# Inverse and transposed inverse in opposite halves of the partitions (a WKV/delta-rule chunk solver on one NeuronCore)

## The chip, the cores and the metric

One core of one Trainium2 chip runs the whole program. The metric is device time of one execution in microseconds; the median of three runs of the kernel before is 2838.22 us (2836.29 to 2838.88).

## What is computed

Two layers of a hybrid block on 256 context and 256 image tokens, all in float32: a mixer with three branches (latent attention, an mLSTM and an RWKV-7 recurrence), a gated merge, and a mixture of 64 experts. The change touches the third branch only. Its reference is a scan over tokens, four heads of 64, forward and backward:

```
def step(s, inp):
    r_t, w_t, k_t, v_t, kk_t, a_t = inp
    sa = jnp.einsum('bhij,bhj->bhi', s, -kk_t)
    s = (s * w_t[..., None, :] + sa[..., :, None] * (kk_t * a_t)[..., None, :]
         + v_t[..., :, None] * k_t[..., None, :])
    return s, jnp.einsum('bhij,bhj->bhi', s, r_t)
```

The kernel computes it in chunks of 64 tokens, for which it needs, per chunk and head, the inverse of a 64x64 unit triangular matrix.

## The kernel before, in words

The 512 tokens are 8 chunks (`NC`) of 64. The four heads are two pairs, `pr` 0 and 1; the two heads of a pair lie in partitions 0 to 63 and 64 to 127 (`each_head`, L908). All tiles of pair 0 have the name `arena` in the profile, those of pair 1 `ring`. `rw_pe` (L911), `rw_act` (L1058) and `rw_dve` (L1121) are the programs of TensorE, ScalarE and VectorE for this branch; each engine runs its own list in order and they meet at semaphores. The branch runs once per layer `l` and direction `d`, so four times.

A product of this branch is 64x64 by 64x64: its operands' partitions choose the rows of the 128x128 array, its output's partitions choose the columns, so it takes one quarter of the array. A float32 product is two MATMUL records, each with its own LDWEIGHTS record; below, one such record is called a pass.

For each `(l, d)`, in this order on TensorE:

- Scores (L947 to L969), masked into `MB` and `MK` by VectorE (L1188).
- The inverse. `X` is the inverse built so far, `XT` its transpose, `NL` the blocks of the matrix that level `v` takes in (`blocks`, L1181). At `v` = 0 TensorE transposes `NL` (L981, with `ident`, 16 products a pair), VectorE makes `X` = I - `NL` (L1195, both operands in SBUF) and `XT` = I - transposed `NL` (L1199, from PSUM). At `v` = 1 to 5 TensorE forms `NL`ᵀ`XT` (L981, 16 products a pair), ScalarE copies it to `ZT` (L1101), and TensorE makes the two updates: L996 for `X` and, at `v` below 5, L998 for `XT`, 16 products each a pair, in the order chunk, head, L996, L998. VectorE subtracts them: `XT` in L1210, `X` in L1212, pair 0 first, then pair 1. L981 of the next level waits for `XT` of its pair (`xt_is`).
- Between L981 and the updates TensorE does a piece of other work, the modulation rows of this or the next layer: `turn` (L326, 8 passes) and `rows` (L313, 16 passes, weights from the DMA ring). Layer 0 has such pieces at all levels, layer 1 `rows` at levels 1 to 3 and `turn` at 1 to 4.
- The scan over chunks, 8 steps. One step: `RH` (L1012, L1013) in each pair, copied with a minus by ScalarE for pair 0 (L1106) and VectorE for pair 1 (L1216); `UU` = `X`·`RH` (L1018), copied (L1108, L1218); the next state (L1024, L1025, L1028), scaled and copied to `ST` (L1112, L1222); the outputs (L1037 to L1039). The next step's L1012 waits for `ST`.

In this kernel every product of the branch has its operands and its output in the same half of the partitions, so only two quarters of the array are ever used: low rows with low columns, and high rows with high columns.

Of the kernel before, what the change touches and what calls it, by code (L numbers as in the profile page):

```python
# [7 lines left out]
ALU = mybir.AluOpType  # L8
# [19 lines left out]
C = 64  # L28
NC = T // C
# [128 lines left out]
def bcast(ap, axis, n):  # L158

    a = ap.unsqueeze(axis)  # L160
    shape = list(a.shape)
    shape[axis] = n
    return a.broadcast_to(shape)


def build(nc, xin, consts, smalls, wsm, wst, wexp, out):
    es = ExitStack()
    with es:
# [22 lines left out]
        ps = [es.enter_context(nc.psum_tensor(f"bank{i}", [P, 512], F32)) for i in range(8)]  # L191
# [11 lines left out]
        def cn(name, n, o=0):  # L203
            return CT[:, CN[name] + o:CN[name] + o + n]
# [4 lines left out]
        ident, ones, bd = cn("ident", P), cn("ones", P), cn("bd", P)  # L209
# [147 lines left out]
        def queries_from(l):  # L357

            return 0 if l == 0 else TC
# [488 lines left out]
        def ring(at, *shape):  # L848
# [3 lines left out]
        NL, ZT, XT, X = ((arena(9224 + 512 * i, T), ring(512 * i, T)) for i in range(4))  # L852
# [4 lines left out]
        AR = (arena(12808, NC, P), ring(2048, NC, P))  # L857
        beta, kappa = ((arena(13832 + 512 * i, T), ring(3072 + 512 * i, T)) for i in range(2))
        VT, BT, KT = ((arena(14856 + 512 * i, NC, 64), ring(4096 + 512 * i, NC, 64)) for i in range(3))
        MB, MK = ((arena(16392 + 1024 * i, NC, P), ring(5632 + 1024 * i, NC, P)) for i in range(2))  # L860

        ST, RH, UU = (tuple(arena(4608 + 256 * i + 128 * pr, 2, 64) for pr in range(2)) for i in range(3))
        hmu, omu = arena(18440, 9), arena(18449, 9)
        LROW = (tsh, arena(12296, T))
        rw, RW = signals("rw", z=9, zev=9, sh=9, tl=2, kc=6, lr=8, sg=8, gc=4, ex=12,
                                                    prep=4, tok=6, tokc=10, sc=16, msk=16, nl=24, pad=1, yd=2, zt=24, ztc=20, xu=20, xd=44,
                                                    step=92, step0=46, step1=46, y=4, yc=4,
                                                    bo=1, bs=2, bc=2, ym=2, yq=2, ys=2, yr=2, g=2, out=2)
# [4 lines left out]
        RH_BANK, UU_BANK, SN_BANK = (4, 3), (5, 7), (6, 2)  # L873
# [15 lines left out]
        def by_chunk(v):  # L889
            return v.rearrange("p (c t) -> p c t", t=C)  # L890
# [17 lines left out]
        def each_head():  # L908
            return (slice(0, 64), slice(64, 128))

        def rw_pe(pe, l):  # L911
            for j in range(9):
                n = CH_RW + j // 4
# [8 lines left out]
            for i in range(2):  # L922
                last = nc.tensor.matmul(ps[4 + i][:, :], bd, YA[:, i, :], start=True, stop=True)
            last.then_inc(rw["kc"], 1)
            pe.wait_ge(rw["tl"], l * RW["tl"] + 2)
            for d in range(2):
# [15 lines left out]
                if d == 0:  # L942
                    pe.wait_ge(rw["kc"], l * RW["kc"] + 4)
                    for pr in PAIRS:
                        for c in range(NC):
                            for h in each_head():
                                last = nc.tensor.matmul(ps[4 + pr][h, c * C:(c + 1) * C], Zs[h, 4 + pr, c * C:(c + 1) * C], ident[h, h], start=True, stop=True)  # L947
# [3 lines left out]
                for pr in PAIRS:  # L951
# [3 lines left out]
                    for b, src in enumerate((beta[pr], kappa[pr])):  # L955
                        for c in range(NC):
                            for h in each_head():
                                last = nc.tensor.matmul(ps[TOK_BANK[pr][b]][h, c * C:(c + 1) * C], src[h, c * C:(c + 1) * C], ident[h, h],
                                                        start=True, stop=True)
# [13 lines left out]
                for v in range(6):  # L973
                    for pr in PAIRS:
                        pe.wait_ge(rw["nl"], l * RW["nl"] + 12 * d + 2 * v + pr + 1)
                        if v:
                            pe.wait_ge(rw["xd"], xt_is(l, d, v - 1, pr))
                        for c in range(NC):
                            for h in each_head():
                                cc = slice(c * C, (c + 1) * C)  # L980
                                last = nc.tensor.matmul(ps[4 + pr][h, cc], NL[pr][h, cc], XT[pr][h, cc] if v else ident[h, h], start=True, stop=True)  # L981
                        last.then_inc(rw["zt"], 1)
                    if v == 0:
                        pe.wait_ge(rw["tokc"], l * RW["tokc"] + 4 * d + 6)
                        continue
                    if v - 1 < len(mods):
                        turn(v - 1)
                    if v < len(mods):
                        rows(v)
                    for pr in PAIRS:  # L990
                        pe.wait_ge(rw["xd"], x_is(l, d, v - 1, pr))
                        pe.wait_ge(rw["ztc"], l * RW["ztc"] + 10 * d + 2 * v + pr - 1)
                        for c in range(NC):
                            for h in each_head():
                                cc = slice(c * C, (c + 1) * C)
                                last = nc.tensor.matmul(ps[pr][h, cc], ZT[pr][h, cc], X[pr][h, cc], start=True, stop=True)  # L996
                                if v < 5:
                                    last = nc.tensor.matmul(ps[2 + pr][h, cc], X[pr][h, cc], ZT[pr][h, cc], start=True, stop=True)  # L998
                        last.then_inc(rw["xu"], 1)
                if len(mods) > 5:  # L1000
                    turn(5)
# [1 line left out]
                for i, c in enumerate(ORDER[d]):  # L1003
                    cc = slice(c * C, (c + 1) * C)
                    for pr in PAIRS:
                        S0 = ST[pr][:, i % 2, :]
                        if i:
                            pe.wait_ge(rw[f"step{pr}"], copied(l, d, i - 1, "sn"))
                        else:
                            pe.wait_ge(rw["xd"], x_is(l, d, 5, pr))  # L1010
                        for h in each_head():
                            nc.tensor.matmul(ps[RH_BANK[pr]][h, 0:64], MK[pr][h, c, 0:64], VT[pr][h, c, :], start=True, stop=False)  # L1012
                            last = nc.tensor.matmul(ps[RH_BANK[pr]][h, 0:64], AR[pr][h, c, 0:64], S0[h, :], start=False, stop=True)  # L1013
                        last.then_inc(rw["step"], 1)
                    for pr in PAIRS:
                        pe.wait_ge(rw[f"step{pr}"], copied(l, d, i, "rh"))
                        for h in each_head():
                            last = nc.tensor.matmul(ps[UU_BANK[pr]][h, 0:64], X[pr][h, cc], RH[pr][h, i % 2, :], start=True, stop=True)  # L1018
                        last.then_inc(rw["step"], 1)
                    for pr in PAIRS:  # L1020
                        S0 = ST[pr][:, i % 2, :]
                        if i < NC - 1:
                            for h in each_head():
                                nc.tensor.matmul(ps[SN_BANK[pr]][h, 0:64], ident[h, h], S0[h, :], start=True, stop=False)  # L1024
                                nc.tensor.matmul(ps[SN_BANK[pr]][h, 0:64], KT[pr][h, c, :], VT[pr][h, c, :], start=False, stop=False)  # L1025
                                if h.start == 0:
                                    pe.wait_ge(rw[f"step{pr}"], copied(l, d, i, "uu"))
                                last = nc.tensor.matmul(ps[SN_BANK[pr]][h, 0:64], BT[pr][h, c, :], UU[pr][h, i % 2, :], start=False, stop=True)  # L1028
                            last.then_inc(rw["step"], 1)
                        else:  # L1030
                            pe.wait_ge(rw[f"step{pr}"], copied(l, d, i, "uu"))
                    for pr in PAIRS:
                        if c * C < queries_from(l):
                            continue
                        S0 = ST[pr][:, i % 2, :]
                        for h in each_head():
                            nc.tensor.matmul(ps[pr][h, cc], S0[h, :], AR[pr][h, c, 64:128], start=True, stop=False)  # L1037
                            nc.tensor.matmul(ps[pr][h, cc], VT[pr][h, c, :], MK[pr][h, c, 64:128], start=False, stop=False)
                            last = nc.tensor.matmul(ps[pr][h, cc], UU[pr][h, i % 2, :], MB[pr][h, c, 64:128], start=False, stop=True)  # L1039
                        if i == NC - 1:  # L1040
                            last.then_inc(rw["y"], 1)
# [79 lines left out]
        def rw_dve(dve, ch, l):  # L1121
# [32 lines left out]
            for d in range(2):  # L1154
# [36 lines left out]
                    dve.wait_ge(rw["msk"], l * RW["msk"] + 8 * d + 8)  # L1191
                    blocks(0, pr)
                for pr in PAIRS:
                    dve.wait_ge(rw["nl"], l * RW["nl"] + 12 * d + pr + 1)
                    nc.vector.tensor_tensor(by_chunk(X[pr]), bcast(cn("eye", 64), 1, NC), by_chunk(NL[pr]), ALU.subtract).then_inc(rw["xd"], 1)  # L1195
                for pr in PAIRS:
                    dve.wait_ge(rw["zt"], l * RW["zt"] + 12 * d + pr + 1)
                    dve.wait_ge(rw["xd"], x_is(l, d, 0, pr))
                    nc.vector.tensor_tensor(by_chunk(XT[pr]), bcast(cn("eye", 64), 1, NC), by_chunk(ps[4 + pr][:, :]), ALU.subtract).then_inc(rw["xd"], 1)  # L1199
                    blocks(1, pr)  # L1200
# [1106 lines left out]
```

## Time and profile before

| | |
|---|---|
| median of 3 runs | 2838.22 us (2836.29 to 2838.88) |
| profiled execution, span from first to last instruction | 2836.5 us |
| mean granted TensorE clock | 0.939 |
| TensorE (PE) busy | 2538.7 us, 90% of the span, 15744 passes |
| weight loads (PEld) busy | 1414.5 us, 50% |
| VectorE (DVE) busy | 836.1 us, 29% |
| ScalarE (ACT) busy | 595.7 us, 21% |

The page gives for the profiled execution no other time than its span, which is 1.7 us under the median of the runs. PE is TensorE's matmul stream, PEld its weight loads; their ends are modelled, so starts are the safer reading. "L981" is line 981 of the kernel. A row of the timeline merges instructions of the same kind: start in us from the span's start, length in us, engine, line, operation, output tile, input tiles, shape and type, count, and in brackets how long the engine was idle before it and what ended that.

### The profile page before, as it was taken

The page shows a single profiled execution, that of the slowest core. Times are in us where ns is not written, and L with a number is a line of the kernel's source. Part 1 is how long each engine was busy: PE and PEld are TensorE (multiplying, and loading weights), DVE is VectorE, ACT ScalarE, POOL GpSimd, SP SyncE. Part 2 cuts the span into 40 slices and gives each one's busy share as a digit, 9 for nine tenths or more (in the row PEclk, how much of TensorE's full clock was granted, in tenths as well). Part 3 has the DMA queues.
Part 4 walks back from the last instruction along what each step waited for, and adds up shares of the span by engine and source line. Part 5 has one row for each costly group of instructions (what it writes and reads, how often), then busy time and mean ns, then how long its engine had stood idle before and what let it go on. Part 6 is the DMA issues. An engine that isn't in the chain of part 4 may idle for free.

```text
span 2836.5 us, 38394 instructions
## 1 busy us (share of the span) xinstructions
PE 2538.7 (90%) x15744; PEld 1414.5 (50%) x15744; DVE 836.1 (29%) x1977; ACT 595.7 (21%) x1176; POOL 170.2 (6%) x178
## 2 busy tenths in 40 slices
PE   6999988999998899899899599988999798888875
PEld 3466557744445544344344356757788533333333
DVE  1254454421114431111111624454411521111114
ACT  3343232120002011111111044333120111111111
POOL 0000000000000111111111000000000011111110
PEclk8999989999997899999999899989999799999997
DMA  7011023422102489999998531112331699999993
GB/s 299 23 60 38 30 79 132 151 90 89 59 0 105 179 342 422 419 393 410 369 406 340 246 143 60 67 56 96 116 154 60 246 380 425 424 418 415 414 399 152
DMA packets 74558, 617.36 MB, mean 218 GB/s; under 512 B 17678, under 2 KB 17678, under 8 KB 32016
## 3 DMA queue, kind: packets, MB, share of 16 engines
q1 hardware_dynamic: 50192, 564.52, 48.8%
q0 software_dynamic: 24192, 50.39, 4.7%
q8 instruction: 125, 2.05, 0.3%
q14 instruction: 49, 0.40, 0.0%
HBM read 604.87 MB, written 47.71 MB: 230 GB/s over the span
## 4 chain that ended last, share of the span: by engine, by line
PE 84%; DVE 6%; issue 4%; DMA 3%; ACT 2%; SPq 0%; POOLq 0%; DVEq 0%; ACTq 0%; POOL 0%
PE bank L1787 22%; PE bank L1802 10%; PE bank L1272 9%; PE bank L296 6%; PE bank L1287 3%; PE bank L1277 3%; PE bank L1777 3%; PE bank L374 3%; PE bank L981 1%; PE bank L996 1%; PE bank L444 1%; PE bank L426 1%; DVE arena L2026 1%; PE bank L313 1%; DMA arena<-expert_rows 1%
## 5 line engine op out<-in xcount | busy, mean ns | idle before, releaser
L1787 PE MATMUL bank<-ring,arena 128*64 128x512 f32 (+1 forms) x1648 | 590.5, 627 | 99.6 <-issue 94.9
L1787 PEld LDWEIGHTS bank<-ring,arena 128*64 128x64 f32 (+1 forms) x1648 | 204.2, 157 | 424.5 <-issue 423.5
L1787 PE MATMUL bank<-branches,arena 128*64 128x512 f32 (+1 forms) x528 | 262.3, 655 | 0.0
L1272 PE MATMUL bank<-normed,ring 128*128 128x512 f32 (+1 forms) x768 | 255.5, 486 | 0.0
L1965 DVE TENSOR_TENSOR arena<-bank,arena 128x256 f32<-128x256 f32 x83 | 35.3, 425 | 706.5 <-ACT arena L1889 706.5
L1711 POOL DMA_INDIRECT arena<-hidden_rows,block_slots x81 | 82.3, 1016 | 2226.5 <-DVE block_slots L1539 1618.1
L1272 PEld LDWEIGHTS bank<-normed,ring 128*128 128x128 f32 x768 | 145.9, 190 | 101.8 <-issue 91.8
L1889 ACT ACTIVATE arena<-bank 128x256 f32<-128x256 f32 x83 | 31.9, 385 | 688.6 <-PE bank L1787 688.6
L296 PE MATMUL bank<-normed,ring 128*128 128x512 f32 (+1 forms) x448 | 173.9, 548 | 0.0
L1802 PE MATMUL bank<-ring,arena 128*64 128x512 f32 (+1 forms) x560 | 163.4, 597 | 1.3 <-DVE arena L1971 1.3
L1802 PE MATMUL bank<-arena 128*64 128x512 f32 (+1 forms) x528 | 140.0, 604 | 1.1 <-ACT arena L1892 1.1
L296 PEld LDWEIGHTS bank<-normed,ring 128*128 128x128 f32 x448 | 84.5, 190 | 84.2 <-issue 81.7
L1971 DVE COPY arena<-bank 128x512 f32<-128x512 f32 x83 | 57.4, 692 | 223.6 <-PE bank L1802 223.6
L1777 PEld LDWEIGHTS bank<-consts,arena 128*128 128x128 f32 x664 | 73.4, 141 | 64.5 <-issue 59.7
L1717 POOL DMA_INDIRECT expert_rows<-arena,block_slots x81 | 80.5, 994 | 351.3 <-ACT arena L1892 227.8
L1802 PEld LDWEIGHTS bank<-ring,arena 128*64 128x64 f32 (+1 forms) x560 | 55.6, 152 | 77.6 <-issue 77.6
L1777 PE MATMUL bank<-consts,arena 128*128 128x128 f32 x664 | 89.1, 277 | 5.7 <-DVE arena L1960 3.5
L1277 PE MATMUL bank<-branches,ring 128*128 128x512 f32 (+1 forms) x256 | 90.4, 486 | 0.0
L1787 PEld LDWEIGHTS bank<-branches,arena 128*64 128x64 f32 (+1 forms) x528 | 80.4, 158 | 16.7 <-issue 16.7
L374 PE MATMUL bank<-normed,ring 128*128 128x512 f32 (+1 forms) x192 | 77.6, 566 | 10.9 <-DMA ring<-in_wst 5.9
L1287 PE MATMUL bank<-arena,ring 128*128 128x512 f32 (+1 forms) x256 | 83.1, 486 | 2.6 <-DVE arena L1316 2.6
L1299 ACT ACTIVATE arena<-bank 128x512 f32<-128x512 f32 (+1 forms) x48 | 23.4, 491 | 286.1 <-PE bank L1272 286.1
(432 smaller groups left out, 3474.3 us busy)
## 6 DMA issues: line engine op xcount, KB each, us to landing
ring<-in_wexp SPq DMA_DIRECT2D x96, 2048.0 KB, 19.6
ring<-in_wst SPq DMA_DIRECT2D x54, 2048.0 KB, 8.5
branches<-in_wexp SPq DMA_DIRECT2D x34, 2048.0 KB, 21.3
ring<-in_wexp SPq DMA_DIRECT2D x66, 1024.0 KB, 21.2
arena<-in_wexp SPq DMA_DIRECT2D x64, 1024.0 KB, 22.3
arena<-expert_rows SPq DMA_DIRECT2D x9, 2048.0 KB, 9.9
ring<-in_wst SPq DMA_DIRECT2D x4, 1536.0 KB, 11.4
branches<-expert_rows SPq DMA_DIRECT2D x3, 2048.0 KB, 16.2
```

The lines of the kernel that those rows point to most:

```text
L296: last = nc.tensor.matmul(bank[:, c0:], weights[:, k, j0:j0 + n], H[:, k, c0:], start=(k == 0), stop=(k == KD - 1))
L374: last = nc.tensor.matmul(ps[j][:, c0:], w[:, k, (j % 4) * P:(j % 4 + 1) * P], H[:, k, c0:], start=(k == 0), stop=(k == KD - 1))
L1272: last = nc.tensor.matmul(ps[2 * (n % 4)][:, c0:], wg[:, k, i * P:(i + 1) * P], H[:, k, c0:], start=(k == 0), stop=(k == KD - 1))
L1277: last = nc.tensor.matmul(ps[2 * (n % 4) + 1][:, c0:], wb[:, k, :], BR[:, k, c0:], start=(k == b0), stop=(k == b1 - 1))
L1287: last = nc.tensor.matmul(ps[m % 4][:, c0:], w[:, k, (m % 4) * P:(m % 4 + 1) * P], YM[:, k, c0:], start=(k == 0), stop=(k == KD - 1))
L1711: pool.indirect_dma_start(XG[s], None, hx[l], bass.IndirectOffsetOnAxis(ap=ids_of[:, u, 0:1], axis=0), bounds_check=TOKENS[l] - 1, oob_is_ ...
L1717: pool.indirect_dma_start(yrows[l], bass.IndirectOffsetOnAxis(ap=ids_of[:, u, 1:2], axis=0), YB[s], None, bounds_check=TOKENS[l] * TOPK - ...
L1777: last = nc.tensor.transpose(ps[h][:, k * P:(k + 1) * P], XG[s][:, (4 * h + k) * P:(4 * h + k + 1) * P], ident)
L1787: last = nc.tensor.matmul(ps[2 + s][r0:r1, :], XT_[:, s, k * P + r0:k * P + r1], wt[:, k, :], start=(k == 0), stop=(k == KD - 1))
L1802: last = nc.tensor.matmul(ps[5 + h][r0:r1, :], HDT[:, s, k * P + r0:k * P + r1], wt[:, k, h * 512:(h + 1) * 512], start=(k == 0), stop=(k ...
L1965: return V.tensor_tensor(SG[:, s, :], ps[2 + s][:, 0:2 * P], SG[:, s, :], ALU.mult)
L1971: return V.tensor_copy(YB[s][:, 512:D], ps[6][:, :])
```

## The change

The inverse `X` of a head is kept in the half of the partitions opposite to the head's own, in which `NL` and `XT` stay; `ZT` goes to the opposite half with it. At `v` = 0 sixteen more products a pair move `NL` to the opposite half through PSUM (`ps[pr]`), and `X` is made from there, after a wait on `zt` where it waited on `nl`. The products of L981 for `v` ≥ 1 and of `RH` write to the opposite half; the two updates read both operands from the opposite half and write one to each half; `UU` reads in the opposite half and writes back in the head's own.

```diff
+        def opposite(h):
+            return slice(64 - h.start, 128 - h.start)
@@ level products (L981)
-                                cc = slice(c * C, (c + 1) * C)
-                                last = nc.tensor.matmul(ps[4 + pr][h, cc], NL[pr][h, cc], XT[pr][h, cc] if v else ident[h, h], start=True, stop=True)
+                                cc, o = slice(c * C, (c + 1) * C), opposite(h)
+                                if v:
+                                    last = nc.tensor.matmul(ps[4 + pr][o, cc], NL[pr][h, cc], XT[pr][h, cc], start=True, stop=True)
+                                else:
+                                    nc.tensor.matmul(ps[4 + pr][h, cc], NL[pr][h, cc], ident[h, h], start=True, stop=True)
+                                    last = nc.tensor.matmul(ps[pr][o, cc], ident[h, h], NL[pr][h, cc], start=True, stop=True)
@@ updates (L996, L998)
-                                last = nc.tensor.matmul(ps[pr][h, cc], ZT[pr][h, cc], X[pr][h, cc], start=True, stop=True)
+                                last = nc.tensor.matmul(ps[pr][o, cc], ZT[pr][o, cc], X[pr][o, cc], start=True, stop=True)
                                 if v < 5:
-                                    last = nc.tensor.matmul(ps[2 + pr][h, cc], X[pr][h, cc], ZT[pr][h, cc], start=True, stop=True)
+                                    last = nc.tensor.matmul(ps[2 + pr][h, cc], X[pr][o, cc], ZT[pr][o, cc], start=True, stop=True)
@@ scan: RH (L1012, L1013) and UU (L1018)
-                            nc.tensor.matmul(ps[RH_BANK[pr]][h, 0:64], MK[pr][h, c, 0:64], VT[pr][h, c, :], start=True, stop=False)
-                            last = nc.tensor.matmul(ps[RH_BANK[pr]][h, 0:64], AR[pr][h, c, 0:64], S0[h, :], start=False, stop=True)
+                            nc.tensor.matmul(ps[RH_BANK[pr]][o, 0:64], MK[pr][h, c, 0:64], VT[pr][h, c, :], start=True, stop=False)
+                            last = nc.tensor.matmul(ps[RH_BANK[pr]][o, 0:64], AR[pr][h, c, 0:64], S0[h, :], start=False, stop=True)
@@
-                            last = nc.tensor.matmul(ps[UU_BANK[pr]][h, 0:64], X[pr][h, cc], RH[pr][h, i % 2, :], start=True, stop=True)
+                            last = nc.tensor.matmul(ps[UU_BANK[pr]][h, 0:64], X[pr][o, cc], RH[pr][o, i % 2, :], start=True, stop=True)
@@ VectorE, v = 0 (L1194 to L1199)
                 for pr in PAIRS:
-                    dve.wait_ge(rw["nl"], l * RW["nl"] + 12 * d + pr + 1)
-                    nc.vector.tensor_tensor(by_chunk(X[pr]), bcast(cn("eye", 64), 1, NC), by_chunk(NL[pr]), ALU.subtract).then_inc(rw["xd"], 1)
+                    dve.wait_ge(rw["zt"], l * RW["zt"] + 12 * d + pr + 1)
+                    nc.vector.tensor_tensor(by_chunk(X[pr]), bcast(cn("eye", 64), 1, NC), by_chunk(ps[pr][:, :]), ALU.subtract).then_inc(rw["xd"], 1)
                 for pr in PAIRS:
-                    dve.wait_ge(rw["zt"], l * RW["zt"] + 12 * d + pr + 1)
                     dve.wait_ge(rw["xd"], x_is(l, d, 0, pr))
```

## Rows read from the trace of the kernel before

**Rows 1.** The page: span, and TensorE's busy time.
```profile
span 2836.5 us, 38394 instructions
PE 2538.7 (90%) x15744; PEld 1414.5 (50%) x15744; DVE 836.1 (29%) x1977; ACT 595.7 (21%) x1176; POOL 170.2 (6%) x178
```

**Rows 2.** Windows over the inverse of layer 0 forward.
```profile
core 0: us, PE busy (x) PEld busy (x) DVE busy (x) ACT busy (x) POOL busy (x), PEclk, DMA share, GB/s
403.69:451.75 48.06, 44.80 (x1080) 35.85 (x1081) 20.39 (x32) 8.96 (x15) 0.00 (x0) 1.00 0.50 183
```

**Rows 3.** Timeline, TensorE, one level (layer 0 forward, updates of level 1).
```profile
411.79 0.34 PE L996 MATMUL bank<-arena 64*64 64x64 f32 x4
...
411.95 0.29 PE L998 MATMUL bank<-arena 64*64 64x64 f32 x4
...
413.70 0.33 PE L996 MATMUL bank<-ring 64*64 64x64 f32 x4
...
415.57 1.15 PE L981 MATMUL bank<-arena 64*64 64x64 f32 x32
...
416.73 1.15 PE L981 MATMUL bank<-ring 64*64 64x64 f32 x32
...
417.81 1.05 PE L326 MATMUL bank<-consts,arena 98*128 98x2 f32 x8
```

**Rows 4.** Timeline, VectorE in the same level.
```profile
414.03 0.69 DVE L1210 TENSOR_TENSOR arena<-arena,bank 128x512 f32<-128x512 f32 x1 [4.24 <-PE bank L998]
...
414.63 0.68 DVE L1212 TENSOR_TENSOR arena<-arena,bank 128x512 f32<-128x512 f32 x1
...
415.89 0.69 DVE L1210 TENSOR_TENSOR ring<-ring,bank 128x512 f32<-128x512 f32 x1 [0.58 <-PE bank L998]
```

**Rows 5.** Timeline, level 0 of layer 0 forward, and the start of level 1.
```profile
403.69 1.15 PE L981 MATMUL bank<-consts,arena 64*64 64x64 f32 x32 [1.52 <-DVE arena L1181]
404.16 0.69 DVE L1195 TENSOR_TENSOR arena<-consts,arena 128x512 f32<-128x512 f32 x1
...
405.36 0.68 DVE L1199 TENSOR_TENSOR arena<-consts,bank 128x512 f32<-128x512 f32 x1
...
406.75 1.15 PE L981 MATMUL bank<-arena 64*64 64x64 f32 x32 [0.97 <-DVE arena L1181]
```

**Rows 6.** Timeline, scan: four passes that one quarter makes alone.
```profile
465.22 0.28 PE L1024 MATMUL bank<-arena,consts 64*64 64x64 f32 x2
465.33 0.28 PE L1025 MATMUL bank<-arena 64*64 64x64 f32 x2
```

**Rows 7.** Timelines: products that share rows but not columns of the array.
```profile
409.96 1.04 PE L313 MATMUL bank<-ring,condv 128*2 128x512 f32 x8
```
```profile
1244.72 0.20 PEld L1787 LDWEIGHTS bank<-ring,arena 128*64 128x64 f32 x4 [0.17 <-issue]
```

**Rows 8.** Line L977, window 407.2 to 407.35: the wait behind L981's first pair.
```profile
L977 PEldq EVENT_SEMAPHORE  x1: 51/51/51, 407.3 to 407.3; - x1
```

**Rows 9.** Timeline, one step of the scan: ScalarE and TensorE.
```profile
466.07 0.31 ACT L1112 ACTIVATE arena<-bank,arena 128x64 f32<-128x64 f32 x1 [0.66 <-PE bank L1028]
...
468.89 0.32 ACT L1112 ACTIVATE arena<-bank,arena 128x64 f32<-128x64 f32 x1 [0.66 <-PE bank L1028]
```
```profile
466.75 0.22 PE L1012 MATMUL bank<-arena 64*64 64x64 f32 x1
...
466.93 0.22 PE L1012 MATMUL bank<-arena 64*64 64x64 f32 x1
```

**Rows 10.** Timeline, layer 0: stalls inside runs of products, forward and backward.
```profile
425.52 0.13 PEld L981 LDWEIGHTS bank<-ring 64*64 64x64 f32 x1
425.55 0.24 PE L981 MATMUL bank<-ring 64*64 64x64 f32 x1
425.58 0.60 ACT L1101 ACTIVATE arena<-bank 128x512 f32<-128x512 f32 x1 [4.23 <-PE bank L981]
...
427.85 1.15 PE L981 MATMUL bank<-ring 64*64 64x64 f32 x31 [2.06 <-issue]
...
535.50 0.33 PE L981 MATMUL bank<-ring 64*64 64x64 f32 x4 [1.71 <-issue]
```

More of the change, by code:

```diff
@@ L994, in rw_pe @@
                             for h in each_head():
-                                cc = slice(c * C, (c + 1) * C)
-                                last = nc.tensor.matmul(ps[pr][h, cc], ZT[pr][h, cc], X[pr][h, cc], start=True, stop=True)
+                                cc, o = slice(c * C, (c + 1) * C), opposite(h)
+                                last = nc.tensor.matmul(ps[pr][o, cc], ZT[pr][o, cc], X[pr][o, cc], start=True, stop=True)
                                 if v < 5:
-                                    last = nc.tensor.matmul(ps[2 + pr][h, cc], X[pr][h, cc], ZT[pr][h, cc], start=True, stop=True)
+                                    last = nc.tensor.matmul(ps[2 + pr][h, cc], X[pr][o, cc], ZT[pr][o, cc], start=True, stop=True)
                         last.then_inc(rw["xu"], 1)
@@ L1011, in rw_pe @@
                         for h in each_head():
-                            nc.tensor.matmul(ps[RH_BANK[pr]][h, 0:64], MK[pr][h, c, 0:64], VT[pr][h, c, :], start=True, stop=False)
-                            last = nc.tensor.matmul(ps[RH_BANK[pr]][h, 0:64], AR[pr][h, c, 0:64], S0[h, :], start=False, stop=True)
+                            o = opposite(h)
+                            nc.tensor.matmul(ps[RH_BANK[pr]][o, 0:64], MK[pr][h, c, 0:64], VT[pr][h, c, :], start=True, stop=False)
+                            last = nc.tensor.matmul(ps[RH_BANK[pr]][o, 0:64], AR[pr][h, c, 0:64], S0[h, :], start=False, stop=True)
                         last.then_inc(rw["step"], 1)
@@ L1017, in rw_pe @@
                         for h in each_head():
-                            last = nc.tensor.matmul(ps[UU_BANK[pr]][h, 0:64], X[pr][h, cc], RH[pr][h, i % 2, :], start=True, stop=True)
+                            o = opposite(h)
+                            last = nc.tensor.matmul(ps[UU_BANK[pr]][h, 0:64], X[pr][o, cc], RH[pr][o, i % 2, :], start=True, stop=True)
                         last.then_inc(rw["step"], 1)
```

## The prediction

> **What bounds the kernel now.** I read the page first: TensorE is busy 90% of 2836.5 us [rows 1]. The branch that changes is a small part of that, so I cut it out with windows. An inverse of one layer and direction, the six levels together, takes 48.1 us in layer 0 forward; TensorE is busy 44.8 of them, at full granted clock, while VectorE has 20.4 [rows 2]. The other three inverses look alike. So TensorE sets the pace of a level, and the timeline says how. The updates of pair 0 start at 411.79, those of pair 1 at 413.70, the next level's L981 at 415.57 [rows 3]. That is 3.78 us for 64 products, or 128 passes. Each of the two quarters in use makes 64 of them, one per 59 ns.
>
> Is 59 ns the price of a quarter or of issuing? In the scan one quarter makes four passes alone: two start at 465.22, the next two at 465.33, so about 57 ns each [rows 6]. A lone quarter has the pace that each of two busy ones has. The quarter is the bound, and twice as many quarters is twice the rate, unless something shared steps in.
>
> **Do quarters with the same rows overlap?** No product of 64x64 shows it. The nearest rows: L313 puts its outputs in four column strips over the same 128 rows. A pass of 512 columns should take eight times 58 ns, 0.46 us, so eight passes one after another 3.7; they lie within 1.04 us [rows 7]. They run four at a time. Four 64-column weight loads of L1787, two per column half over the same rows, fit in 0.20 us, while a single one is 0.13 [rows 7, 10]: loads overlap too. And order: the program has for each head L996 and then L998, two passes each; the trace shows four L996 passes and then four L998 [rows 3]. The second head's L996 overtakes the first head's L998, so a free quarter isn't held up by a busy one.
>
> The Trainium skill ("TensorE: Matmul & The Clock Gate", Part 3, "The mechanism") says the opposite: matmuls start strictly in program order, and a weight load overlaps a running matmul only where the row groups differ. By that rule the updates would keep their 3.78 us and the time would be that of the second rival below. The trace disagrees on both points, in the rows just named.
>
> **Updates, levels 1 to 4.** Each quarter gets 16 passes a pair: 0.94 us, 1.87 for both pairs. Against issuing: the wait of L977 stands behind 64 instructions (32 loads, 32 passes) and came at 407.3, where the first of their passes started at 406.75 [rows 5, 8]: some 9 ns an instruction, 18 a pass. Four quarters want one pass per 14.6 ns. At 18 the updates would take 2.3 us; but a part is queued already during the modulation rows ahead of them, so I take 2.0.
>
> What is late next is VectorE. Now XT of pair 0 starts 0.33 us after the point where pair 1's products take over (413.70 to 414.03), the next operation 0.60 later, and L981 of pair 1 starts 0.84 after XT of pair 1 (415.89 to 416.73); L326 follows 1.08 later [rows 3, 4]. With the start of the updates as zero: XT of pair 0 at 0.94 + 0.33 = 1.27, L981 of pair 0 at 2.11; X at 1.87, XT of pair 1 at 2.47 (its products are ready by 2.33), L981 of pair 1 at 3.31, L326 at 4.39. Today L326 comes at 417.81 - 411.79 = 6.02. So 1.63 us are gained a level, not 1.87, and the 2.0 of issuing is hidden in it. The copies to ZT stay under L326 and L313. Where layer 1 has neither (level 5), ZT of pair 0 is ready some 0.9 us after its last pass (0.25 to the copy, 0.60 the copy, as L1101 has it [rows 10]), when L981 of pair 1 is just done: no loss. Four levels, four times: 16 x 1.63 = **26.1 us less**. Bounds: 1.2 if 18 ns a pass holds throughout and VectorE waits for it, 1.87 if VectorE's order costs nothing; 19 to 30 us.
>
> Level 5 has only L996, in two quarters as before: nothing. L981 of later levels only moves to the other two quarters: same count, same pace, nothing.
>
> **Level 0.** Added are 16 products a pair, so 64 passes instead of 32. In four quarters that is 0.94 us a pair, at the issuing pace 1.15. X was made from SBUF at 404.16, under the transposes [rows 5]; it now waits for them. X of pair 0: 403.69 + 0.94 + 0.33 = 404.96. X of pair 1, after twice 0.94: 405.90. XT of pair 0 follows 0.60 later, 406.50, against 405.36 now [rows 5]: 1.14 us later, and by the issuing pace 1.6. Behind it in VectorE's list stand the blocks of level 1, for which L981 at 406.75 waits [rows 5], so all of it is on the path. I take 1.4, four times: **5.6 us more** (4.6 to 6.4). The operand in PSUM costs nothing: L1195 takes 0.69 from SBUF, L1199 0.68 from PSUM [rows 5]. No DMA is added; POOL's and SP's lists are untouched.
>
> **Scan.** RH and UU leave the two quarters in which the state and the outputs run. One step is 2.82 us (L1112 at 466.07 and 468.89) [rows 9]. ST of pair 0 is ready at 466.38, yet RH starts at 466.75 in one quarter and at 466.93 in the other, behind the outputs of the step before [rows 9]. In free quarters it could start near 466.43: 0.5 us less at most. If a product can overtake only a few others, RH still starts in both quarters when the first is free, 0.18 less; a gain of nothing is the lower bound. No row shows how many can be overtaken; the shown cases pass two to six passes. I take 0.3, nearer to those. Seven borders between steps, four times: 28 x 0.3 = **8.4 us less** (0 to 14).
>
> **Instruction supply.** At 425.55 TensorE stopped for 2.06 us inside a run of products, waiting for nothing that the profile names, and again for 1.71 us ahead of 535.50 [rows 10]. Both fall in inverses in which the DMA engines are half busy [rows 2]. A TensorE that uses up its instructions faster can meet more of that. I add **2 us** (0 to 10).
>
> **Sum.** -26.1 + 5.6 - 8.4 + 2 = -26.9 us. The profiled execution's span is 1.7 us under the median of the runs; taken off the median, 2838.2 - 26.9 = **2811.3 us**. What follows the branch starts earlier as a whole: the weights of a level, 2.1 MB in 7.2 us, need 290 GB/s where the inverse now moves 183 with half of the DMA time free [rows 2]. With the bounds of its terms the case's own range is 2800 to 2828.
>
> **Rivals.**
> 1. *Issuing bounds it.* If a pass costs 25 ns to issue, the updates take 128 x 25 ns less 0.3 queued ahead, 2.9 us; L326 comes at 2.9 + 0.33 + 0.84 + 1.08 = 5.15, a gain of 0.87; level 0 costs 2.5. Sum -13.9 + 10 - 8.4 = -12.3: 2826. For it: passes never come denser than 29 ns on average now. Against: rows 8 give 18. Chance 8%. (The Trainium skill, same page, Part 1, states a floor of about 25 ns from start to start for small matmuls; no run shown comes so low on average.)
> 2. *Slower: quarters with the same rows take turns.* The place is the row side of the array, for operands or loads. Then the updates keep 3.78, and level 0, doubled, costs 1.87 a pair: XT at 403.69 + 3.74 + 0.33 + 0.60 = 408.4, 3.0 late, four times 12; the scan gains nothing. 2850. It decides once a pair's 64 update passes need more than about 1.7 us, where the levels no longer pay for level 0. For it: no 64-row products overlap this way so far. Against: rows 7. Chance 9%.
> 3. *Stalls like those of rows 10 multiply.* Eight more of 2 us: 2811 + 15 = 2826. For it: both known ones fall where DMA is busy. Against: only two in four inverses. Chance 6%.
> 4. *Given back.* Levels wait for their weights, or gain and level 0 cancel: within 0.2% of 2838. Against: the free half of the DMA time [rows 2]. Chance 7%.
>
> **Numbers.** The forecast gets 70%. 0.2% (5.7 us) is about what a measurement of this kernel can tell from no change. Faster: 70 + 8 + 6 = 84%; within: 7%; slower: 9%. The range 2800 to 2828 holds the forecast's own bounds and rivals 1 and 3.
>
> **What would show it.** Levels: updates of both pairs in about 2.0 us where rows 3 have 3.78, and L326 4.4 us after their start. Level 0: L1199 1.1 to 1.7 us later behind the first L981 than now. Scan: L1112 every 2.3 to 2.6 us. The prediction is wrong if the updates still take over 3 us, if level 0 costs 3 us, or if idle time put down to "issue" inside L981, L996 or L998 grows by more than 10 us.

## The result and the profile after

The changed kernel takes 2855.65 us (median of 5 runs, 2849.28 to 2860.06) against 2838.22 (2835.14 to 2842.52): ratio 1.0057, 95% interval 1.0043 to 1.0072. It is 17.4 us slower; I had forecast 26.9 us less. A cut of the trace by stages puts all of it in the branch that was edited: from the branch's first projection to its last output 270.8 us become 281.0 in layer 0, 238.6 become 247.4 in layer 1, 19.0 together. The span of the profiled executions grows by 16.1 us, since the stages ahead of the branch, which were not edited, took 3.6 us less in this one; the same stages differ by up to 7 us between the profiles of this document. All tables and windows below come from one profiled execution of each kernel.

The page after, to hold beside [rows 1]: fewer busy microseconds on TensorE, 16 us less of them, and a longer span.

```profile
span 2852.6 us, 38898 instructions
PE 2522.6 (88%) x16000; PEld 1392.8 (49%) x16000; DVE 836.0 (29%) x1977; ACT 595.1 (21%) x1176; POOL 170.2 (6%) x178
```

So work was saved and idle time was bought. The window over the inverse of layer 0 forward (first pass of level 0 to first pass of the scan) is to be held beside [rows 2]; its columns are the same. [Rows 2] end 1 us earlier, at 451.75; up to the first pass of the scan (452.73) the inverse before took 49.04 us, of which TensorE was busy 45.78.

```profile
400.04:454.10 54.06, 43.79 (x1152) 31.41 (x1153) 20.98 (x33) 8.96 (x15) 0.00 (x0) 0.91 0.46 168
```

TensorE makes more passes in less busy time, but idles 10.3 us instead of 3.3, and its granted clock is 0.91 where it was 1.00. Two losses, then: gaps and clock. Three parts of the timeline show what the change did and where the gaps are.

**The updates**, timeline of TensorE behind the modulation rows, as in [rows 3]. L1004 and L1006 were L996 and L998:

```profile
409.23 0.27 PE L1004 MATMUL bank<-arena 64*64 64x64 f32 x1
409.24 0.27 PE L1006 MATMUL bank<-arena 64*64 64x64 f32 x1
409.25 0.27 PE L1004 MATMUL bank<-arena 64*64 64x64 f32 x1
409.25 0.27 PE L1006 MATMUL bank<-arena 64*64 64x64 f32 x1
409.34 0.22 PE L1004 MATMUL bank<-arena 64*64 64x64 f32 x1
...
411.37 1.15 PE L986 MATMUL bank<-arena 64*64 64x64 f32 x32
412.56 1.00 PE L986 MATMUL bank<-ring 64*64 64x64 f32 x27
...
416.72 0.58 PE L986 MATMUL bank<-ring 64*64 64x64 f32 x5 [3.16 <-issue]
417.23 1.86 PE L326 MATMUL bank<-consts,arena 98*128 98x2 f32 x8
...
419.02 1.03 PE L313 MATMUL bank<-ring,condv 128*2 128x512 f32 x4
```

All four quarters start within 20 ns, and both pairs' updates (128 passes) are over in 1.88 us from first start to last, 14.7 ns a pass, where [rows 3] had 3.78. Then, five passes before the end of L986 (L981 before), TensorE stands still for 3.16 us, put down to "issue"; [rows 10] had two such stalls in layer 0, and here layer 0 has five. Behind the stall everything is slow: the first four passes of L313 take 1.03 us, where four take 0.61 at the full clock.

**Level 0**, timeline of VectorE (L1205 writes X, L1208 XT, L1191 the blocks), the first product of level 0 (L988; L989 is the added one) and the first of level 1, to hold beside [rows 5]:

```profile
400.04 0.27 PE L988 MATMUL bank<-consts,arena 64*64 64x64 f32 x1 [1.52 <-DVE arena L1191]
...
401.27 0.69 DVE L1205 TENSOR_TENSOR arena<-consts,bank 128x512 f32<-128x512 f32 x1 [0.68 <-PE bank L989]
402.20 0.69 DVE L1205 TENSOR_TENSOR ring<-consts,bank 128x512 f32<-128x512 f32 x1 [0.24 <-PE bank L989]
402.81 0.68 DVE L1208 TENSOR_TENSOR arena<-consts,bank 128x512 f32<-128x512 f32 x1
403.40 0.69 DVE L1191 TENSOR_TENSOR arena<-arena,consts 128x512 f32<-128x512 f32 x1
...
404.19 0.51 PE L986 MATMUL bank<-arena 64*64 64x64 f32 x10 [2.06 <-DVE arena L1191]
```

Level 1 starts 4.15 us behind the first pass of level 0, before 3.06; TensorE waits 2.06 us for VectorE instead of 0.97.

**The clock behind these waits.** Windows over the same 88 passes behind level 0, in the four inverses of the changed kernel (columns: window, its length, busy time of the engines, then the granted clock):

```profile
404.20:409.20 5.00, 5.00 (x88) 3.29 (x88) 2.47 (x4) 1.19 (x2) 0.00 (x0) 1.00 0.01 3
508.40:514.70 6.30, 6.27 (x88) 4.72 (x88) 2.52 (x4) 1.19 (x2) 0.00 (x0) 0.73 0.01 3
1911.40:1917.70 6.30, 6.27 (x88) 4.72 (x88) 2.51 (x4) 1.19 (x2) 0.00 (x0) 0.73 0.01 3
2003.50:2009.80 6.30, 6.30 (x88) 4.69 (x88) 2.48 (x4) 1.20 (x2) 0.00 (x0) 0.73 0.01 3
```

In three of four inverses part of the stretch runs at the lower level (1.2 GHz instead of 2.4), and it takes 1.3 us longer. The same two levels are seen behind the first stall above (window 417.2 to 424.8):

```profile
417.20:424.80 7.60, 7.60 (x153) 4.44 (x152) 1.27 (x2) 1.19 (x2) 0.00 (x0) 0.59 0.20 45
```

**What arrives in a stall.** The DMA view of the stretch up to the middle of the first stall, and of 1.1 us behind it (queue, packets, MB, share of the 16 engines):

```profile
q1 hardware_dynamic: 77, 1.26, 94.5%
```
```profile
q1 hardware_dynamic: 29, 0.48, 103.8%
q8 instruction: 1, 0.02, 5.0%
```

From 410.4 to 414.1 the engines carry nothing but packets of the weight transfer that SP had asked for at 409.36, when the modulation rows had freed its buffer. The next packet of the instruction queue comes at 414.2, and TensorE goes on at 416.72, 2.5 us after it. Such a packet holds 16 KB, and the stalls begin at counts of TensorE's instructions that lie a multiple of 256 apart (4033 and 5313 here; 4289 for the first one of [rows 10]). That is no accident of three: in the four inverses of the 13 profiles of this document (before, after and the experiments) there are 85 stalls of 0.4 us or more put down to "issue", and every one lies at such a count. An inverse passes some nine of these counts. Of the 34 in the kernel before, 3 have a stall; of the 35 in the changed kernel, 11. And in eight of the nine stalls of over 1 us in the changed kernel TensorE goes on 2.2 to 2.5 us after the start of the last instruction packet (3.2 in the ninth), as behind both stalls of [rows 10] (2.3). In the updates 256 instructions (128 loads, 128 passes) last 1.9 us now and lasted 3.8 before; a weight transfer occupies the engines for some 7.2 us from its first packet to its last.

The four inverses together, read from the first pass of level 0 to the first of the scan:

| part | before | after | difference |
|---|---|---|---|
| four inverses | 181.5 | 203.2 | +21.7 |
| of it, 16 undisturbed levels (8.83, 7.22 each) | | | -25.8 |
| level 0 (0.97, 2.06 idle) | 3.9 | 8.2 | +4.4 |
| other idle time of TensorE over 0.3 us | 4.8 | 26.0 | +21.3 |
| rest: products at the lower clock | | | +21.8 |
| four scans | 88.4 | 85.5 | -2.9 |

The last row but one is what is left over; the windows above show 3.9 of it behind level 0. The trace agrees with its size: the granted clock is at the lower level for 51 us of the four inverses, 49 of them busy, where the kernel before has 3.4, all busy. Work done at half the clock takes twice its time, so the 46 us more account for some 23 (an estimate).

### The profile page after: what moved, and what is told of

Read it like the earlier page. It is cut to its first block, busy times and chain, and to the rows that moved or that the text cites. A ratio compares the mean times of both kernels' runs of the same rounds, so it can differ in the third digit from the quotient of the medians.

```text
span 2852.6 us, 38898 instructions
## 1 busy us (share of the span) xinstructions
PE 2522.6 (88%) x16000; PEld 1392.8 (49%) x16000; DVE 836.0 (29%) x1977; ACT 595.1 (21%) x1176; POOL 170.2 (6%) x178
## 4 chain that ended last, share of the span: by engine, by line
PE 83%; DVE 6%; issue 5%; DMA 3%; ACT 2%; SPq 0%; POOLq 0%; ACTq 0%; DVEq 0%; POOL 0%
PE bank L1796 21%; PE bank L1811 10%; PE bank L1281 9%; PE bank L296 6%; PE bank L1296 3%; PE bank L1286 3%; PE bank L1786 3%; PE bank L374 3%; PE bank L986 2%; PE bank L313 1%; PE bank L444 1%; PE bank L426 1%; DVE arena L2035 1%; PE bank L1004 1%; PE bank L404 1%
## 5 line engine op out<-in xcount | busy, mean ns | idle before, releaser
L1796 PE MATMUL bank<-branches,arena 128*64 128x512 f32 (+1 forms) x528 | 247.7, 625 | 0.0
## 6 DMA issues: line engine op xcount, KB each, us to landing
ring<-in_wexp SPq DMA_DIRECT2D x66, 1024.0 KB, 21.8
arena<-in_wexp SPq DMA_DIRECT2D x64, 1024.0 KB, 21.3
```

Of the source, the lines that this page charges most:

```text
L1796: last = nc.tensor.matmul(ps[2 + s][r0:r1, :], XT_[:, s, k * P + r0:k * P + r1], wt[:, k, :], start=(k == 0), stop=(k == KD - 1))
```

## The experiments

My theory after these rows: the update does what it should; the loss is level 0's order and, above all, an instruction supply that falls behind when the weight transfer and the denser run of instructions coincide, each wait taking the clock down after it. The main rival: the idle time comes from the four quarters themselves, which use up instructions too fast whatever the DMA engines do.

**1. Small transfers, in the kernel before and in the changed one.** In both:

```diff
-sp.dma_start(in_slot(slot(m, j))[:, 0:CH_COLS[j]], wst[m, j, :, 0:CH_COLS[j]])...
+n = 256 if is_late(m, j) else CH_COLS[j]
+sp.dma_start(in_slot(slot(m, j))[:, 0:n], wst[m, j, :, 0:n])...
```

Kernel before:

> The kernel before, but of each late modulation chunk only 256 of 4096 columns are transferred (128 KB instead of 2 MB); TensorE multiplies whatever lies in the rest of the slot, so the modulation values, and the result with them, are others. Theory (a large weight transfer holds up TensorE's instruction fetch): the stalls of 2.06 and 1.71 us inside L981 go, with the slow-clock stretch behind the second; some 5 us less than before, about 2833. Rival (TensorE uses up its instructions faster than they can be delivered, whatever the DMA queues do): stalls stay, no change, 2838.

Changed kernel:

> The changed kernel with the same cut of the late modulation transfers (the modulation values, and the result, are others). Theory (large transfers hold up the fetch): idle time of over 0.3 us inside the four inverses falls from 34 us to the 4 x 2.06 of level 0; the inverses last 41.7, 41.7, 35.4 and 35.5 us where the changed kernel has 54.1, 55.4, 47.8 and 46.0; the time is about 2806 to 2812. Rival (consumption is simply too fast for the supply): stalls of 2 to 4 us stay in L986 and the time stays within 5 us of the changed kernel's 2855.

Measured: 2896.61 us (2890.74 to 2900.43) and 2883.83 (2881.03 to 2886.75). Both are longer than the full kernels in a later stage: the experts of layer 1 take 628 and 625 us instead of 561 and 560, presumably because other modulation values route the tokens otherwise. So only the pair says something: with small transfers the change is 12.8 us faster, not 17.4 slower. The inverses take 174.6 and 166.0 us. The two of layer 0 in the changed kernel came as expected (41.5 and 41.7 us), the two of layer 1 did not (39.5 and 43.4, expected 35.4 and 35.5). The groups of L986 (here L991) by the idle time ahead of them, in the changed kernel and then in the changed kernel with small transfers (the numbers behind the bar: busy time, mean ns, idle before):

```profile
L986 PE MATMUL bank<-ring 64*64 64x64 f32 x640 | 28.7, 247 | 12.9 <-issue 12.0 <-DVE ring L1219 0.4
L986 PE MATMUL bank<-arena 64*64 64x64 f32 x640 | 26.2, 233 | 19.8 <-issue 11.2 <-DVE arena L1191 8.2
```
```profile
L991 PE MATMUL bank<-ring 64*64 64x64 f32 x640 | 25.1, 228 | 1.5 <-issue 0.6 <-DVE ring L1224 0.3
L991 PE MATMUL bank<-arena 64*64 64x64 f32 x640 | 24.4, 224 | 13.8 <-DVE arena L1196 8.2 <-issue 5.0
```

"Issue" goes from 23.2 to 5.6 us; the 8.2 behind VectorE (level 0) stay. Most of what is left is one stall of 4.3 us in the last inverse, inside a 2 MB transfer of the next stage, which was not made small; it has the lower clock behind it, as has the wait at level 0 in the third inverse. The rival falls: the same products in the same quarters stall little once the transfers are short. The experiment takes away length and bytes of the transfers together and doesn't say which of them matters.

**2. The same bytes in four transfers, one behind another.**

```diff
-sp.dma_start(in_slot(slot(m, j))[:, 0:CH_COLS[j]], ...)
+n = CH_COLS[j] // 4 if is_late(m, j) else CH_COLS[j]
+for at in range(0, CH_COLS[j], n):
+    sp.dma_start(in_slot(slot(m, j))[:, at:at + n], ...)
```

> The kernel before, each late modulation chunk moved in four transfers of 1024 columns, so in rows of 4 KB instead of 16 KB, same bytes at the same moment. Theory with the wait at the engines' already accepted 16 KB pieces: the fetch waits a quarter as long, the stalls go, about 2833. Theory with the wait for the whole transfer: as before, 2838. Rival (supply too slow in itself): 2838.

> The changed kernel with the same four transfers of 4 KB rows. Wait at the accepted 16 KB pieces: the fetch lands about 1 us into a burst instead of 3.9, stalls in L986 go, the inverses last about 42 (layer 0) and 36 us (layer 1), 2808 to 2815 in all. Wait for the whole transfer: no change, 2855. Rival (supply too slow in itself): no change, 2855.

Measured: 2841.12 us (ratio 1.0003, 0.9987 to 1.0019) and 2853.39 (1.0053, 1.0031 to 1.0074). Asked for at once, four transfers follow one another without a gap, as one does. Inverses 186.5 and 201.2 us: no cure, and in the profile of the kernel before 5 us more, which its time doesn't show.

**3. Four transfers, each behind a semaphore of the level**, so that gaps open between them; and for comparison one whole transfer that only starts once L986 of the next level is done.

```diff
+for at, gate in enumerate([None] + gates(l, late)):
+    if gate:
+        sp.wait_ge(*gate)
+    sp.dma_start(in_slot(slot(m, j))[:, at * n:at * n + n], ...)
```

> The changed kernel; the late weight chunks (and the first two of the merge) come in four transfers of 512 KB, asked for at four moments spread over the level. Theory (what matters is how much of a transfer lies ahead of the fetch): a fetch waits under 2 us, the stalls go but for level 0's 2.06; inverses about 42 us in layer 0 and 36 in layer 1 as in the run with cut transfers, 2806 to 2815 in all. Rival (total use of the DMA engines): stalls stay, 2850 or more, since the four short transfers of a_split changed nothing.

> The kernel before with the same four spread transfers. Theory: its few stalls go, inverses 46.5 us in layer 0 and 41 in layer 1; 2830 to 2835. This is the fair partner of a_pieces: their difference is what the four quarters are worth once the fetch is out of the way, by the timeline 16 x 1.6 - 4 x 1.1 + 3 for the scan = 24 us. Rival: 2838.

> The changed kernel; each late weight chunk is one 2 MB transfer as before, but SyncE asks for it only after the next level's L986 is done, so that a transfer begins under the modulation rows (48 instructions in 2.8 us) and not under the updates (256 in 1.9 us). Theory (a fetch asked for during a transfer arrives some 5 us after the transfer's beginning, and TensorE has 256 instructions in hand): stalls shrink from 2 to 4 us to under 2, inverses of layer 0 near 45 us, 2825 in all. Rival (the stalls come from the total use of the DMA engines, which this leaves alone): no change, 2855.

Measured: changed kernel with pieces 2841.34 us (1.0000, 0.9982 to 1.0019); kernel before with pieces 2833.55 (0.9976, 0.9963 to 0.9988); changed kernel with the delay 2840.51 (1.0010, 0.9995 to 1.0024). Against the changed kernel's 1.0057, pieces and delay each give back about 14 us, so when a transfer starts matters, with its bytes unchanged. That is far short of the expected 40 to 50 us (pieces) and 30 (delay), and with pieces in both kernels the change still costs 7.8 us where it was expected to gain 24. Neither ends the stalls: the inverses take 191.6 and 191.4 us, with 17.3 and 17.1 us idle beyond level 0. (The profile of the kernel with the delay is that of its slowest run, 2853.59 us, so its 191.4 and 17.1 may be above what is usual.) Why, the DMA view of the kernel with pieces shows, from 418 to 444 us (queues, then issues with the median us to landing):

```profile
q1 hardware_dynamic: 1715, 6.24, 74.0%
q8 instruction: 4, 0.07, 1.0%
issues: line engine op xcount, KB each, median us to landing
ring<-in_wst SPq DMA_DIRECT2D x11, 512.0 KB, 5.2
```

A level of 7.2 us asks for a chunk whose transfer takes 7.2 us. The pieces fall behind their gates and run together again, 5.2 us from issue to landing. In the kernel before, a level is 8.8 us; in the same stretch its pieces land after 4.0 us, and its inverses come down to 175.9, all but undisturbed. That the wider spacing is what saves it there fits these numbers but was not tried by itself. The free half of the DMA time, on which I had built, is not there for a faster level: the engines are some 80% busy inside a transfer, but already in the trace of before one transfer takes 7.1 us from its first packet to its last (421.70 to 428.81), about the length of the new level.

**4. Level 0 in another order**: VectorE writes XT and its blocks ahead of X.

```diff
 for pr in PAIRS:
-    X[pr] = eye - ps[pr]
-for pr in PAIRS:
     XT[pr] = eye - ps[4 + pr]
     blocks(1, pr)
+for pr in PAIRS:
+    X[pr] = eye - ps[pr]
```

Alone, on the changed kernel:

> The changed kernel with nothing else than level 0 put in another order: VectorE writes XT and its row blocks ahead of X, so that level 1 starts behind the transposes' evictions. In the traces of the changed kernel level 1 starts 4.15 us after the first pass of level 0 and TensorE idles 2.06 us there; the kernel with pieces and this order idled 0.34 to 0.53 us. Theory (the loss has two parts, the order at level 0 and stalls of the instruction supply behind weight transfers): the order gives back 4 x 1.3 = 5 us and leaves the stalls, so 2848 to 2852 us, still slower than before or level with it, and the issue gaps of 2 to 4 us remain. Rival 1 (the order is the whole loss of the change, and the rest of the difference lies elsewhere): well under 2838 us. Rival 2 (the gaps only move: with level 1 earlier by 1.3 us, an instruction fetch meets a transfer in other places): anywhere from 2840 to 2860 us, with issue gaps whose sum differs by several us from the 26 us of the changed kernel.

With small transfers:

> The changed kernel with small late modulation transfers (256 columns of a chunk; the modulation values are then other ones) and the new order of level 0. To be compared with the same kernel without the order (2883.8 us) and with the kernel before with small transfers (2896.6 us). Theory: without long transfers the whole of the change and of the order show: 4 x 1.3 us off, 2878 us, that is 0.6% under the kernel before with small transfers; the stage of the inverses is 5 us shorter in each layer's two directions together or less by one stall. Rival (something else than the transfers limits the inverse): no gain over 2883.8 us.

Measured: 2846.08 us (12 runs, 1.0021, 1.0006 to 1.0035), 9.6 less than the changed kernel; and 2877.60 (2873.93 to 2881.90), as expected, 6.2 less than without it. The first gain looks like twice what I expected of the order, but the two intervals together leave some 4 to 16 us, so 5 is not excluded, and neither is the second rival (the gaps move), into whose range 2846 falls as well. The timeline has level 1 start behind a wait of 0.53 us, and the windows show a gain in clock beside it:

```profile
400.63 0.94 PE L986 MATMUL bank<-arena 64*64 64x64 f32 x23 [0.53 <-DVE arena L1191]
```
```profile
400.60:405.60 5.00, 4.97 (x88) 3.41 (x88) 3.52 (x6) 1.19 (x2) 0.00 (x0) 1.00 0.01 3
502.60:507.60 5.00, 5.00 (x88) 3.29 (x88) 3.48 (x6) 1.19 (x2) 0.00 (x0) 1.00 0.01 3
1900.40:1905.40 5.00, 5.00 (x88) 3.27 (x88) 3.47 (x6) 1.19 (x2) 0.00 (x0) 1.00 0.01 3
1990.80:1995.80 5.00, 4.99 (x88) 3.29 (x88) 3.49 (x6) 1.19 (x2) 0.00 (x0) 1.00 0.01 3
```

The same 88 passes run at the full clock in all four inverses. So in these two profiles level 0 cost 4 x 1.5 us of waiting and 3 x 1.3 us of clock, 9.9 together. How often the clock falls there varies from run to run: over the five profiles with the wait of 2.06 us it fell behind 13 of 20 such waits. The stalls stay (21.9 us idle beyond level 0), as the theory had it. This profile is that of the fastest of the twelve runs (2836.78 us), and its inverses are 17 us shorter than those of the changed kernel, so 9.9 is not a measure of the median.

The small-transfer kernel in this order is the clearest look at what the change is worth by itself:

```profile
399.00:445.60 46.60, 45.55 (x1094) 36.68 (x1089) 20.88 (x36) 8.96 (x15) 0.00 (x0) 1.00 0.06 17
```
```profile
400.30:441.20 40.90, 39.18 (x1154) 29.86 (x1155) 20.64 (x33) 8.96 (x15) 0.00 (x0) 1.00 0.07 20
```

These are the first inverse of the kernel before with small transfers and of this one: 46.6 and 40.9 us, both at the full clock. All four: 174.6 and 151.7. The edited branch as a whole, both layers: 508.4 and 479.6 us, 28.8 less. The kernel as a whole gains less: the medians, 2896.61 and 2877.60, differ by 19.0 us and the two profiled spans by 20.0. Outside the branch the second profile is 8.8 us longer (3.4 ahead of it, 2.7 between the layers, 2.7 behind), in stages that were not edited. Likewise the changed kernel with small transfers but without the new order has 14.3 us more in its inverses, but only 6.2 in its median. So a branch time of one profile is uncertain by several microseconds, and 19.0 is what was measured of the gain.

**5. Pieces and order together**, in the hope of a version that beats both.

> As a_pieces, and at level 0 VectorE makes XT and the blocks of level 1 ahead of X, which is needed only two operations later. Theory (level 0 costs 1.1 us more in the changed kernel because X stands ahead of XT in VectorE's list): L986 of level 1 starts 1.2 us earlier in each of the four inverses, 5 us less than a_pieces, 2801 to 2810. Rival: it waits for the doubled products themselves: no change against a_pieces.

> The same kernel as the one with pieces and the new order, once more and with more rounds, since only four runs gave its 2821.8 us (2816 to 2842). Theory: it holds within 5 us, at 2817 to 2828 us, faster than before by 0.4 to 0.8%, because both parts of the loss are made smaller: the order by 5 us and the stalls by some. Rival: the four runs were lucky; pieces alone gave no gain over the kernel before (2841 us), so 2836 us with the 5 us of the order.

Measured: first 2821.83 us from only four runs (2816.16 to 2841.63; 0.9927), then, over twelve, 2835.81 (2826.71 to 2849.73; 0.9987, 0.9971 to 1.0003). The second expectation's rival was right: the first four were lucky. Inverses 184.9 us, 20.6 idle beyond level 0. It is 20 us better than the changed kernel and level with the kernel before. The expected sum of both cures, 2801 to 2810 us, was not reached either time. The fastest kernel whose gain is certain remains the kernel before with pieces, 0.24% faster, without the change.

## Why the prediction was wrong

**Updates (-26.1): right.** 16 x 1.61 = 25.8 by the undisturbed levels, and L986 starts 2.13 us behind the updates in them, where 2.11 was forecast. Quarters with the same rows overlap fully, as [rows 7] had suggested; rival 2 is out. The issuing price of 18 ns a pass from [rows 8] was wrong, 14.7 ns was reached, and it made no difference, because VectorE sets the rest of the level. The Trainium skill's rule ("TensorE: Matmul & The Clock Gate", Part 3) that matmuls start in program order and loads overlap only across row groups does not hold in this trace (L1004 and L1006 alternate pass by pass, where the program has two passes of the one and then two of the other, and 128 loads of some 0.13 us lie within the same 1.9 us), nor does the floor of about 25 ns from start to start (Part 1).

**Level 0 (+5.6): the delay right, its price short.** The delay measured 1.09 us each, 4.4 in all. That the clock can fall behind the longer wait, here three times at 1.3 us, was not in the sum: 8.3 together.

**Scan (-8.4): mis-sized, -2.9.** In layer 0 forward L1122 comes every 2.67 us (461.51, 464.18), where [rows 9] had 2.82. The timeline of the products at such a border:

```profile
462.13 0.22 PE L1048 MATMUL bank<-ring 64*64 64x64 f32 x1
462.14 0.28 PE L1021 MATMUL bank<-arena 64*64 64x64 f32 x2
462.19 0.22 PE L1048 MATMUL bank<-ring 64*64 64x64 f32 x1
462.25 0.22 PE L1021 MATMUL bank<-arena 64*64 64x64 f32 x1
462.25 0.22 PE L1049 MATMUL bank<-ring,arena 64*64 64x64 f32 x1
462.26 0.22 PE L1021 MATMUL bank<-arena 64*64 64x64 f32 x1
462.30 0.22 PE L1022 MATMUL bank<-arena 64*64 64x64 f32 x1
462.31 0.22 PE L1049 MATMUL bank<-ring,arena 64*64 64x64 f32 x1
```

The state is ready at 461.82, yet RH starts at 462.14, when three passes of the outputs are left; in the kernel before it was three as well. So the lower mechanism that I had named holds: both quarters now start at once (0.18), and no earlier. Of that 0.15 remains a step in layer 0, since the first pass in a quarter that had been idle takes longer (L1021 from 462.14 to its second at 462.25). Layer 1 makes outputs for only part of its steps, has less to overtake, and gains 0.05 to 0.08 a step on average. I had counted 28 equal borders.

**Instruction supply (+2, at most 10): this is the step that failed.** I had seen both stalls of [rows 10] and had put down rival 3 (they multiply) with 6% and a size of 16 us. What happened is rival 3 at about two and a half times that size: 21.3 us more idle time and, without level 0's share, some 18 at the lower clock. That is over the term's own bound of 10, and the sign of being wrong that the prediction named ("issue" time inside these lines up by more than 10 us) came. I missed three things that the trace of before held. The stalls sit inside weight transfers, and a transfer begins in most levels (16 in the four inverses), so there were many occasions, not two. The supply comes in portions of 256 instructions, which the change uses up in half the time, just at the point where the transfer starts. And TensorE's clock can fall behind a stall: in the trace of before it was at the lower level from 536.3 to 539.7 behind the stall of 1.71 us, though not behind that of 2.06. In the changed kernel each microsecond of stall cost nearly two. (Apart from the failed step: the upper bounds of the terms added give 2835.6, not the 2828 that the range ends at; 2855.65 lies beyond both.) The Trainium skill ("Runtime: NRT & Kernel Launch", "Instruction fetch mechanics") describes these 16 KiB blocks of 256 instructions and calls the crossing from one to the next "mostly hidden"; in this case's traces it is hidden at 31 of 34 crossings before and at 24 of 35 after, and the long stalls lie in or just behind a weight transfer. Experiment 1 carries this: with the long transfers gone the loss turns into a gain. Experiment 3 shows that the moment of a transfer counts; the clock's share is read from the windows. How the instruction queue and the weight packets share the DMA engines was not tried by itself; that the packet lands late inside a transfer is what the views show.

**The sum.** Of what I forecast for the branch without the supply term (-28.9), the small-transfer kernels show -10.3 in the branch as changed (-12.8 in the medians), and -28.8 with level 0 in the better order (-19.0 in the medians). The agreement of -28.8 with -28.9 is in part luck: it is one pair of profiles, and the forecast had no better order in it and too much for the scan. The reasoning about quarters was sound; the bound had moved to a resource that I had read as half free.

## What to carry to other kernels

A faster inner stretch raises the demand for everything that feeds it. Before counting the gain of denser products, divide a portion of the instruction supply and the weight bytes of the stretch by its new length: if transfers then fill the DMA engines without a gap, small "issue" stalls in the old trace are the first sign of the next bound. And price each new wait of TensorE at its length plus the products that may follow at the lower clock; here that nearly doubled it.

## What was not expected of the hardware

- 64x64 products in four quarters: 128 passes with 128 loads in 1.88 us, 14.7 ns a pass, which is the pace of four quarters at 59 ns each.
- TensorE stalls of up to 4.2 us with nothing named but "issue", while a 2 MB weight transfer holds the DMA engines at 94% and more; in the stall shown, the 16 KB instruction packet starts only 3.9 us after the transfer begins. All 85 stalls of 0.4 us and more lie at counts of TensorE's instructions a multiple of 256 apart.
- A wait of 2.06 us at level 0 was followed by the lower clock in 13 of 20 cases (6.3 us for 88 passes instead of 5.0 where windows were read); a wait of 0.97 us in none of 16, and one of 0.53 us in none of 8 (the kernels with pieces and order, where a stall follows at once, left out).
- At the borders of the scan read here, in both kernels, the overtaking product starts when three passes are left in the quarter that is still busy; in the changed kernel its own quarter had been free before.
